# A mixer and expert kernel on one core: the first tile's gates in a strand of their own, two heads' scores in one PSUM bank, and token norms applied after the products

## The reference, cut to what matters

```python
h = rmsnorm(x, mix_norm_g)                       # per token: h = x * rsqrt(mean(x^2)) * g
qa, ka, va, qd, kd, vd, qm, graw = split(h @ w_in)
gates = sigmoid(graw)                            # 3 x 1024 per token
mem_n = rmsnorm(mem, mem_norm_g); mk, mv = split(mem_n @ w_mem_kv)
o_a, o_d, o_m = causal(qa, ka, va), dilated(qd, kd, vd), memory(qm, mk, mv)   # 6, 6 and 4 heads of 64
merged = gates[0] * (o_a @ w_a) + gates[1] * (o_d @ w_d) + gates[2] * (o_m @ w_m)
x = x + merged @ w_out
x = x + (silu(u_gate) * u_val) @ w_ffn_down      # u = causal_conv3(rmsnorm(x) @ w_ffn_up)
for l in range(2):                               # second block
    mixed = concat(forgetting_attention, conformer_conv, rglru)(rms_norm(x) @ w_in_2[l])
    x = x + mixed @ w_out_2[l]
    xn = rms_norm(x); 8 heads choose 16 of 16384 experts each per token
    x = x + sum_k gate_k * gelu(xn . U[e_k]) * V[e_k]
x = rms_norm(x)
```

## Time and profile before

| | |
|---|---|
| median of 3 runs | 2147.11 us (2147.04 to 2147.55) |
| profiled execution | 2146.26 us, of which 2144.5 us from the first to the last instruction |
| TensorE busy | 1746.1 us (81%), 6904 matmul records |
| VectorE busy | 1348.5 us (63%) |
| ScalarE busy | 807.3 us (38%) |
| GpSimd busy | 595.3 us (28%) |
| moved by DMA | 774.29 MB, mean 361 GB/s |
| chain that ended last | TensorE 40%, DMA 34%, VectorE 14%, issue 5%, ScalarE 4%, GpSimd 3% |

### The profile page before, as it was taken

How to read it: one execution, slowest core, us unless ns; L and a number is a source line. 1 busy time by engine, 2 the same in 40 slices (tenths; PEclk the granted TensorE clock), 3 DMA queues, 4 the chain that set the end, 5 groups by cost and what they waited for, 6 DMA issues and landing times.

```text
span 2144.5 us, 21045 instructions
## 1 busy us (share of the span) xinstructions
PE 1746.1 (81%) x6904; PEld 1012.3 (47%) x6904; DVE 1348.5 (63%) x3432; ACT 807.3 (38%) x2104; POOL 595.3 (28%) x516
## 2 busy tenths in 40 slices
PE   7988989889878888977767877767798777677776
PEld 3447847547567464453324633623364362222222
DVE  2423314713988558757886786588888658885444
ACT  2232201520456436523434354134437414333333
POOL 0000000000222223533444353234443324434331
PEclk9989999799989999989989898978999988879999
DMA  9556767157999999999999999999999998999997
GB/s 359 214 199 235 290 241 293 50 229 263 385 417 406 418 414 407 416 420 406 410 409 418 411 412 402 419 361 419 420 419 420 419 378 321 394 383 415 420 420 311
DMA packets 108526, 774.29 MB, mean 361 GB/s; under 512 B 12160, under 2 KB 12416, under 8 KB 16256
## 3 DMA queue, kind: packets, MB, share of 16 engines
q0 software_dynamic: 73728, 536.90, 61.2%
q1 hardware_dynamic: 34688, 236.04, 27.8%
HBM read 771.85 MB, written 1.05 MB: 360 GB/s over the span
## 4 chain that ended last, share of the span: by engine, by line
PE 40%; DMA 34%; DVE 14%; issue 5%; ACT 4%; POOL 3%; SPq 0%; DVEq 0%; POOLq 0%; ACTq 0%
DMA kv<-in_peer_dram,eidx 12%; PE psum L1070 10%; DMA arena<-in_peer_dram,eidx 10%; PE psum L723 8%; PE psum L737 8%; DMA ring<-in_slabs_dram 7%; PE psum L927 5%; DMA ring<-in_peer_dram,eidx 4%; PE psum L945 3%; POOL arena L2082 1%; DVE arena L1931 1%; PE psum L902 1%; DVE kv L1931 1%; DVE x L1941 1%; DMA wf<-in_wf_dram 1%
## 5 line engine op out<-in xcount | busy, mean ns | idle before, releaser
L1070 PE MATMUL psum<-arena,diag 128*128 128x512 f32 x824 | 425.5, 651 | 127.9 <-ACT diag L1393 124.8
L2082 POOL DMA_INDIRECT arena<-in_peer_dram,eidx x258 | 306.3, 1187 | 479.3 <-PE psum L1070 367.6
L1931 DVE CUSTOM_DVE_ANT_0 arena<-arena,osb 128x1024 f32<-128x1024 f32 x258 | 314.0, 1223 | 163.4 <-DMA arena<-in_peer_dram,eidx 162.7
L2082 POOL DMA_INDIRECT kv<-in_peer_dram,eidx x130 | 147.8, 1137 | 828.5 <-DVE eidx L1802 534.0
L1383 ACT ACTIVATE wexp<-hid 128x1 f32<-128x1 f32 x512 | 103.0, 201 | 702.4 <-DVE hid L1931 701.6
L1070 PEld LDWEIGHTS psum<-arena,diag 128*128 128x128 f32 x824 | 159.2, 206 | 355.0 <-ACT diag L1393 198.8
L1070 PE MATMUL psum<-kv,diag 128*128 128x512 f32 x428 | 219.0, 640 | 60.7 <-ACT diag L1393 56.7
L723 PE MATMUL psum<-ring,hT 128*128 128x512 f32 x560 | 252.0, 603 | 4.4 <-DMA ring<-in_slabs_dram 1.6
L1070 PE MATMUL psum<-ring,diag 128*128 128x512 f32 x376 | 197.0, 654 | 71.5 <-ACT diag L1393 71.3
L1931 DVE CUSTOM_DVE_ANT_0 kv<-kv,osb 128x1024 f32<-128x1024 f32 x130 | 158.6, 1222 | 82.4 <-DMA kv<-in_peer_dram,eidx 81.9
L737 PEld LDWEIGHTS psum<-hT,ring 128*128 128x128 f32 x1536 | 184.3, 199 | 34.6 <-DMA ring<-in_slabs_dram 18.1
(11 more groups left out here) (315 smaller groups left out, 1794.1 us busy)
## 6 DMA issues: line engine op xcount, KB each, us to landing
ring<-in_slabs_dram SPq DMA_DIRECT2D x206, 1024.0 KB, 6.9
ring<-in_slabs_dram SPq DMA_DIRECT2D x8, 768.0 KB, 5.5
arena<-in_peer_dram,eidx POOLq DMA_INDIRECT x258
ring<-in_slabs_dram SPq DMA_DIRECT2D x8, 512.0 KB, 4.3
kv<-in_peer_dram,eidx POOLq DMA_INDIRECT x130
kk<-in_keys_dram SPq DMA_DIRECT2D x2, 1024.0 KB, 11.0
ring<-in_peer_dram,eidx POOLq DMA_INDIRECT x124
rowg<-in_rows_dram SPq DMA_DIRECT2D x3, 512.0 KB
```

The source lines that it names most:

```text
L1070: ins = pe.matmul(bank(b), diags_of(n), pair(slot_of[n])[:, 1024 + 512 * h:1536 + 512 * h], start=(k == 0), stop=(k == 127))
L1931: v.tensor_tensor_reduce(out=row, in0=row, in1=row_y[t], scale=1.0, scalar=0.0, op0=ALU.mult, op1=ALU.add, accum_out=hid[:, c:c + 1]).then ...
L2082: pool.indirect_dma_start(pair(i), None, tables, bass.IndirectOffsetOnAxis(ap=eidx[:, 128 * t + k:128 * t + k + 1], axis=0)).then_inc(sig. ...
```

## The change

1. The six gate products of tile 0 leave B0's `weave` and become a stage G0, second in `STAGES`, with its own steps on TensorE, ScalarE and in the list of slabs. The planner places them. Each waits for its bank through `after`, and B0's branch products wait for all six.
2. In every stage the scores of the two heads of a unit lie in one bank (2 times 256 columns), so each S has two sets; after the first head TensorE waits for its own product to be complete. B0 also gets two banks for T and for O, M01, M10 and M11 two for T.
3. In B0, B1 and for the memory, x and mem are transposed as they are. The norm is applied as the `scale` of ScalarE's copies out of PSUM and of the sigmoids. `xs`, `mem_s` and their three kinds of VectorE multiply are gone. The mixers and the feed-forward keep their scaling ahead of the transposes.

```diff
-            "B0": Room(range(8), (0, 6), (2,), (4,), scr, hT, tmp),
-            "M00": Room((0, 1, 2, 3, 0, 1, 2, 3), (0,), (2,), (3,), ...),
-            "B1": Room((4, 5, 6, 7, 4, 5, 6, 7), (4,), (6,), (7,), scr, hT, tmp),
+            "B0": Room(range(8), (0, 1), (2, 6), (4, 7), scr, hT, tmp),
+            "M00": Room((0, 1, 2, 3, 0, 1, 2, 3), (0, 1), (2,), (3,), ...),
+            "B1": Room((4, 5, 6, 7, 4, 5, 6, 7), (4, 5), (6,), (7,), scr, hT, tmp),
...
-            room[m] = Room((4, 5, 1, 3, 4, 5, 6, 7), (4, 6), (1,), (3,), scr, hT, tmp)
+            room[m] = Room((4, 5, 1, 3, 4, 5, 6, 7), (4, 6), (1, 5), (3,), scr, hT, tmp)
...
-        STAGES = ("B0", "M00", "R00", "C00", "B1", ...
+        STAGES = ("B0", "G0", "M00", "R00", "C00", "B1", ...
...
                 def scores(i):
                     u, n = units[i], r.S[i % len(r.S)]
-                    s3 = psum[:, 512 * n:512 * n + 1024].rearrange("p (h k) -> p h k", h=2)[:, :, 0:u.nk]
+                    s3 = bank(n).rearrange("p (h k) -> p h k", h=2)[:, :, 0:u.nk]
                     for done in ready:
                         w.wait_ge(*done)
+                    wait_bank(n)
                     for h in range(2):
-                        wait_bank(n + h)
                         ins = pe.matmul(s3[:, h, :], u.q(h), u.k(h), start=True, stop=u.bias is None)
                         if u.bias is not None:
                             ins = pe.matmul(s3[:, h, :], *u.bias(h), start=False, stop=True)
+                        if h == 0:
+                            ins.then_inc(*own.up())
+                            w.wait_ge(*own.now())
...
-                yield from turn_tile(s, scr_[:, 0:1024], b_[6:8], "turned_v", at("scaled", s, "h"), "h")
+                yield from turn_tile(s, x3[:, t, :], b_[6:8], "turned_v", (sig.sem("l_x%d" % t), 16), "h")
...
-                        yield from turn_tile(s, mem_s[:, u, :], b_[6:8], "turned_v", at("mem_scaled", 1), "m%d" % u)
+                        yield from turn_tile(s, mem3[:, u, :], b_[6:8], "turned_v", (sig.sem("l_m"), 16), "m%d" % u)
...
-                if t == 0:
-                    yield from weave(heads(), gate_chunks())
-                else:
-                    yield from heads()
+                yield from heads()
...
+                    if t == 0:
+                        w.wait_ge(*at("gates_out", t, 5))
...
+            def first_gates():
+                b_, hTt = room["B0"].bank, hT_tile("B0")
+                w.wait_ge(*at("turned_v", "B0", "h", 1))
+                for c in range(6):
+                    after = at("gates_out", 0, c - 2) if c > 1 else at("mem_out", 1, 1) if c else at("turned_v", "B0", "h", 1)
+                    yield from token_tile("G0", (b_[5], b_[3])[c % 2], hTt, "gates", 0, c, after=after)
...
+                    w.wait_ge(*at("rms", s))
                     for i, (d, of) in enumerate(pieces(s, t, c)):
-                        act.activation(d, bank(b_[c % 2])[:, of], ACT.Copy).then_inc(*up("qkv_out", t, c, i))
+                        act.activation(d, bank(b_[c % 2])[:, of], ACT.Copy, scale=sm[:, 641 + 3 * t:642 + 3 * t]).then_inc(*up("qkv_out", t, c, i))
...
-                y = yield from rms_tile(s, "h")
-                w.wait_ge(*own.now())
-                v.tensor_scalar(xs, x3[:, t, :], y, None, ALU.mult).then_inc(*up("scaled", s, "h"))
+                yield from rms_tile(s, "h", "rms", s)
```

More of the change, by code:

```diff
@@ L1268, in block, with first_gates @@
                 for _ in range(22):
+                    yield
+            def first_gates():
+                b_ = room["B0"].bank
+                for c in range(6):
+                    w.wait_ge(*at("gates", 0, c))
+                    w.wait_ge(*at("rms", "B0"))
+                    act.activation(gates[:, c // 2, 512 * (c % 2):512 * (c % 2) + 512], bank((b_[5], b_[3])[c % 2]), ACT.Sigmoid,
+                                   scale=sm[:, 641:642]).then_inc(*up("gates_out", 0, c))
                     yield
@@ L2132, in block @@
                     yield
-                    for c in range(6):
-                        slab(S_GATE + c)
-                        yield
                     for br in range(3):
@@ L2156, in block, with first_gates @@
                     yield
+            def first_gates():
+                for c in range(6):
+                    slab(S_GATE + c)
+                    yield
             def mixer(l, t):
```

82 lines of the change are left out of this document (32 added, 50 removed).

## The result

The kernel became slower: the median of 20 runs is 2154.16 us (2148.79 to 2159.79) against 2144.19 us of 20 runs of the kernel before on the same chips, a ratio of 1.0046 [1.0036, 1.0057]. The forecast was 2134 us with 0.75 on faster. The profiled execution took 2151.74 us, 2149.9 of them from the first to the last instruction. That is 5.5 us more than the profiled execution of before (2146.26), where the medians differ by 10.0; so one profile of each kernel places about half of the loss; the rest is placed by no profile.

A forecast was written before the change was run, and what follows sets the result against it. Computation was taken to bound the kernel up to the first gather, bytes behind it. B0's 9.0, a net 0 and B1's 4.1 gave 13.1 us; 2146.3 less that is 2133.2, the median 0.85 above: 2134 us, range 2117 to 2151.

The forecast's parts named there:

- What bounds the kernel: Up to the first gather the chain of computation sets the time, behind it the bytes; some 68 us are lost.
- The strand, 9.0 us: In B0, gate products fall into the attention's waits: 7.5 us gained, plus 1.5 from a higher TensorE clock.
- six gate slabs behind the memory slab: In B0's slab queue, moving these loads behind the memory slab costs 0, since DMA is busy 58% and 18%.
- The wait between heads: TensorE's wait between a unit's two heads costs 0 to 0.3 us each; 2.4 us in all in B0.
- The norm in B1, 4.1 us: At B1's start the norm leaves the path: products start near 299.5 in place of 305.54, gaining 4.1 us.
- Second sets: In B1 and M00, second score sets gain 1.5 us (0 to 4.7), cancelled by 1.5 us of new waits.
- ScalarE's copies: Copies scaled by the norm cost between 0 and a second pass of 0.60 us; 0 was taken.
- C: Rival: heads in B0 and B1 lose an overlap, 4 us, and B0 gives 3 rather than 9; 2140 to 2144; chance 0.15.
- E: Rival: slower, the VectorE bubble at tile boundaries comes twice more or twice as long, 28 us; 2162 us; chance 0.13.
- over 13 us at more than two places: Sign of a wrong forecast: GpSimd waits this long before gathers, pointing to D or E.
- D: Rival: the gain is given back behind the first gather by one more wait like 13.4 us; 2147 us; chance 0.10.
- The table load: In B0, two more loads at 1.28 us each; the skill's rule would make them cost 2.8 us more.

The follow-up runs named there:

- multiply_first: Changed kernel with part 2 undone, M00's first turn not put behind B1, and in B1 VectorE's multiply into hT ahead of the norm; 0.9989 of the kernel before.
- strand_only: Changed kernel with parts 2 and 3 undone, so the kernel before with the gate strand alone; 0.9966 of the kernel before.
- pairs_all: multiply_first with all 105 pairs pinned that VectorE adds to x in strand_only, in every tile; 0.9962 of the kernel before.
- strand_44: strand_only with VectorE adding 44 pairs in the last tile in place of 8; 0.9961 of the kernel before.
- changed_old_banks: Changed kernel with part 2 undone: scores in two banks, no wait between heads; 0.9997 of the kernel before.
- norms_only: Kernel before with part 3 alone, the norms behind the products; 1.0036 of the kernel before.
- banks_only: Kernel before with part 2 alone, though by an oversight tile 0's gate sigmoids keep the norm's scale, so its output is wrong; 1.0081 of the kernel before.
- before_wait: Kernel before, same order and banks, with only the wait between the two heads' products added to every unit; 1.0079 of the kernel before.
- before_44: Kernel before with VectorE adding 44 pairs in the last tile in place of 8; 0.9974 of the kernel before.

## Why the prediction was wrong

**What bounds the kernel: right.** Rate and bytes behind the first gather are as before, the waits at the boundaries too (13.40 and 14.39 us), and the 4.95 us that the changed kernel loses at the first expert numbers are 5.4 us in the span of its profiled execution. "A microsecond saved ahead of the first gather is a microsecond at the end" holds only while the plan behind it stays: multiply_first gave back 11 of 13.6 us, and with its pairs pinned as in strand_only (pairs_all) it went from 0.9989 to 0.9962.

**The strand, 9.0 us: right.** strand_only: 8.1 us at the completion of x, 10.8 at the first expert numbers (5.9 in strand_44, the same up to there), 7.3 us by the ratio. VectorE's head norm resumes at 71.21 after the root (71 to 73 was forecast), and the branch products take 13.99 us in the changed kernel ("some 15"). One cost was missed: the six gate slabs behind the memory slab, priced at 0 since the DMA had room, cost a wait of 6.96 us at 73.26. strand_only has it too (6.97 us at 71.81) and gains all the same. Room on the DMA was the wrong row to look at: with three places in the ring the order of the slabs sets when one can be asked for. In the changed kernel 5.3 of the 9 us arrive. Against strand_only it loses 2.8 us, and changed_old_banks, without the waits, already 2.4: its first 80 records take 37.51 us against 36.09, its branch products 17.01 against 15.84. The waits hold the output's turn back by 3.3 us (128.91 against 125.61), and the branch products behind it, at full clock again, take 3.0 us less.

**The wait between heads: the step that failed.** "Above, the nearest row is a handoff from another engine ... so 0 to 0.3" measured 0.54 and 0.75 us. The round trip of 0.28 was priced rightly. What was left out is the overlap of the heads, and it was left out for the wrong comparison: 0.42 us for four records of 128 columns beside 0.44 of four transposes. What one head takes alone would have been the measure, and that is 0.41: the two ran wholly beside each other even there. The prediction's own rows could have warned of it: it used 0.59 us for a pair of 256 columns, and its gate rows say 0.43 for one record of 512, so 0.86 for the pair one after another. All eight units of B1 are of that size. So B0 pays 6 x 0.54 + 2 x 0.75 = 4.7 us where 2.4 were set, and B1's eight units 8 x 0.75 = 6.0, where 1.5 were set for it and M00 and cancelled against 1.5 of gain. The sum had part 2 at a cost of 2.4 us; it measured 10.5, by the ratio of the changed kernel to changed_old_banks.

**The norm in B1, 4.1 us: failed in its order.** "A turn and the multiply into hT let the products start near 299.5" overlooked that VectorE's program has the whole norm ahead of that multiply: the products begin 5.75 us after x is complete and not 2.8. "M00's turn now cuts in with 1.94" didn't happen either: with its wish of 1.3 it was picked only behind B1's products, which are ready earlier than before, and the hole of 20 us followed. That a stage becomes ready earlier was taken as a gain without asking what the plan then puts first. The term of 4.1 us of gain measured a loss of 7.7 us, 0.36%, in norms_only. Made as predicted, in multiply_first, the step brings B1's products 2.4 us behind x without a hole.

**Second sets, ScalarE's copies.** No run shows the 1.5 us of the second sets by themselves; banks_only, which has them, is no faster than before_wait, which hasn't (1.0081 and 1.0079). A scaled copy of 512 columns takes 0.69 us in place of 0.60, well under the second pass that was the bound.

**The rivals.** C came true in one half, the lost overlap, and beyond its size: it allowed 4 us for it, in a kernel that would have ended at 2144. Its other half, a strand that gives only 3 us, did not. E, the side on which the result lies, had the wrong mechanism; the boundaries are unchanged. It also read them wrongly: "two show the bubble", but GpSimd waits 13.40 us before the gather at 995.30 of before too, near the third boundary, and 13.29 us before that at 1171.11. So "over 13 us at more than two places" could not tell D or E from the kernel before. What D says, a gain given back behind the first gather, wasn't seen in the changed kernel but in multiply_first, and there not by one more such wait. What no case held was two small failures in the same 250 us: a mispriced wait and a changed order.

**The table load.** The rule of the Trainium skill, "ScalarE: Activation LUTs", section "What ACT_TABLE_LOAD costs", that a drain adds 1.38 us is again not seen: in B1 of the changed kernel the load at 293.60 takes 1.28 us and the root begins at 294.89, 0.01 us behind its end.

**The best version.** strand_only, strand_44 and pairs_all all lie at 0.996, faster than both kernels; the first is the simplest, and is part 1 of the change alone.

## What to carry to other kernels

Before two products on different rows of the array are put into one bank, look at when the records of the two start, at the largest size that occurs: if they start together, a wait between them costs its round trip and the overlap. The time of the pair beside that of other products, as the prediction had it, can miss this. When a stage becomes ready earlier in a kernel whose order is planned, read in the new order what the engine does at that moment and what is left for its next wait: here eight transposes picked behind eighty records in place of ahead of them left TensorE idle for 20 us, and more was lost than the norm's way out of the path had saved. And divide a change before it is judged: here one part of three was worth 0.34%, and the other two hid it.

## What the runs showed of the hardware that wasn't expected

- A wait of TensorE for its own last product costs 0.28 us in a row of full-height products, and 0.54 (128 columns) or 0.75 us (256) between two float32 products on different halves of the rows.
- Two heads' float32 products on different halves of the rows, written to two banks, start 6 to 7 ns apart and take no longer together than one alone: 0.63 us at 256 columns, 0.42 against 0.41 at 128. A record of 256 columns lasts 428 ns on average when alone (changed kernel), and the pair at 376.60 of before has the same durations, 480 and 376 ns. The mean of 542 ns in before's group comes from its units at the lower clock.
- ScalarE's copy from PSUM took 0.09 us more with its scale from memory: 0.69 for 0.60 at 512 columns. The first line is of the changed kernel, the second of before:

```profile
306.40 0.69 ACT L1199 ACTIVATE scr<-psum,sm 128x512 f32<-128x512 f32 x1 [11.22 <-PE psum L727]
```

```profile
313.26 0.60 ACT L1190 ACTIVATE scr<-psum 128x512 f32<-128x512 f32 x1 [12.77 <-PE psum L723]
```

- TensorE's clock follows what it did before: the products behind two turns back to back ran at 0.95, behind one turn, 4.20 us of idle time and one turn at 0.50 for 6 us. In before_wait the twenty units took 17 us more of TensorE, where at full clock the waits would add 10 x 0.54 + 10 x 0.75 = 12.9 (an estimate, M00's four priced like B0's): more of the attention around them stood at the lower level.
- A last tile with 44 of its pairs added by VectorE has a lower clock on TensorE (0.79 in place of 0.92 in before_44's last 340 us) and isn't slower for it; the DMA share there is 0.96.
